# Recurrence of a hybrid layer: the next head's gates and logs one level phase sooner, and the coarsest level's differences inside ScalarE's exponentials

## What is computed

```python
def chunk_recurrence(q, k, v, log_a, s0):
    """S_t = diag(a_t) S_{t-1} + k_t v_t^T ; o_t = S_t^T q_t, chunkwise."""
    ...
    def step(state, blk):
        qc, kc, vc, la = blk
        b = jnp.cumsum(la, axis=2)
        rel = b[:, :, :, None, :] - b[:, :, None, :, :]
        decay = jnp.exp(jnp.where(causal, rel, -jnp.inf))
        ...
            scores = jnp.einsum('bhtsd,bhsd->bhts', qc[:, :, :, None, :] * decay, kc)
        out = (jnp.einsum('bhts,bhsv->bhtv', scores, vc)
               + jnp.einsum('bhtd,bhdv->bhtv', qc * jnp.exp(b), state))
...
def hg_dir(p, z, lb):
    q = jax.nn.silu(to_heads(p[4], HG_HEADS))
    f = lbh + (1.0 - lbh) * jax.nn.sigmoid(to_heads(z, HG_HEADS).astype(jnp.float32))
    return q, 1.0 - f, to_heads(p[7], HG_HEADS), jnp.log(f)
```

## Time and profile before

| what | us |
|---|---|
| median of 3 runs (2803.54 to 2812.65) | 2808.24 |
| the profiled execution | 2807.85 |
| its span, first to last instruction | 2806.2 |
| TensorE busy in the span | 2599.8 |
| VectorE busy | 2061.4 |
| ScalarE busy | 1457.5 |
| GpSimd busy | 587.0 |

### The profile page before, as it was taken

How to read it: one execution, slowest core, us unless ns; L and a number is a source line. 1 busy time by engine, 2 the same in 40 slices (tenths; PEclk the granted TensorE clock), 3 DMA queues, 4 the chain that set the end, 5 groups by cost and what they waited for, 6 DMA issues and landing times. The chain is left out here.

```text
span 2806.2 us, 45616 instructions
## 1 busy us (share of the span) xinstructions
PE 2599.8 (93%) x16249; PEld 2213.0 (79%) x16250; DVE 2061.4 (73%) x2465; ACT 1457.5 (52%) x1498; POOL 587.0 (21%) x457
## 2 busy tenths in 40 slices
PE   7989887999797999999999999999999999999994
PEld 3887665767786789777887978799989897888783
DVE  5265787563665897999879787866686778877884
ACT  5255557212533664776557465544454546645553
POOL 0055666300022211122122111111121112111110
PEclk9998888999898999999999999999999999999997
DMA  7121112171343896999879787866686769967863
GB/s 289 47 69 30 35 33 62 57 260 62 102 104 113 329 380 212 368 355 354 302 234 362 245 302 263 281 202 207 194 295 206 255 228 335 322 210 271 299 229 135
DMA packets 274720, 605.90 MB, mean 216 GB/s; under 512 B 21869, under 2 KB 53013, under 8 KB 273521
## 3 DMA queue, kind: packets, MB, share of 16 engines
q1 hardware_dynamic: 254256, 561.62, 56.2%
q0 software_dynamic: 20384, 43.19, 6.9%
HBM read 582.09 MB, written 46.97 MB: 224 GB/s over the span
## 5 line engine op out<-in xcount | busy, mean ns | idle before, releaser
L2404 ACT ACTIVATE whi<-e_slot 128x2048 fp32r<-128x2048 f32 x296 | 561.0, 1912 | 438.0 <-PE e_acc L2330 370.7
L2466 DVE TENSOR_TENSOR e_slot_r<-e_slot,whi 128x2048 fp32r<-128x2048 f32 x296 | 674.7, 2286 | 101.9 <-ACT whi L2404 101.9
L2327 PE MATMUL e_acc<-e_xhi,whi 128*128 128x256 f32 x1664 | 399.4, 282 | 3.2 <-ACT e_xhi L2408 3.2
L2404 ACT ACTIVATE whi<-slot 128x2048 fp32r<-128x2048 f32 x148 | 283.2, 1914 | 194.1 <-PE e_acc L2302 194.1
L2466 DVE TENSOR_TENSOR slot_r<-slot,whi 128x2048 fp32r<-128x2048 f32 x151 | 344.7, 2285 | 19.5 <-ACT whi L2404 16.5
L2244 POOL DMA_INDIRECT sum<-yo,e_idx_now x50 | 122.4, 2447 | 1014.5 <-issue 541.5
L2300 PE MATMUL e_acc<-whi,e_ahi 128*128 128x512 f32 x800 | 319.3, 399 | 0.0
L2327 PEld LDWEIGHTS e_acc<-e_xhi,whi 128*128 128x128 f32 x1664 | 313.1, 188 | 6.3 <-ACT e_xhi L2408 6.3
L2302 PE MATMUL e_acc<-whi,e_alo 128*128 128x512 f32 x800 | 313.4, 392 | 0.0
L2301 PE MATMUL e_acc<-e_slot_r,e_ahi 128*128 128x512 f32 x800 | 311.5, 389 | 0.0
L2300 PE MATMUL e_acc<-whi,e_xhi 128*128 128x512 f32 x768 | 303.3, 395 | 0.2
(11 more groups left out here) (407 smaller groups left out, 5059.2 us busy)
## 6 DMA issues: line engine op xcount, KB each, us to landing
e_slot<-in_w SPq DMA_DIRECT2D x296, 1024.0 KB, 8.1
slot<-in_w SPq DMA_DIRECT2D x151, 1024.0 KB
rv<-in_w_ada SPq DMA_DIRECT2D x32, 512.0 KB, 5.2
slot<-in_w_in SPq DMA_DIRECT2D x9, 1024.0 KB, 9.9
wa<-in_w_ada SPq DMA_DIRECT2D x8, 1024.0 KB, 17.3
slot<-in_w_in SPq DMA_DIRECT2D x12, 512.0 KB, 4.6
xt<-in_x SPq DMA_DIRECT2D x8, 512.0 KB, 15.0
slot<-in_w_out SPq DMA_DIRECT2D x4, 1024.0 KB, 13.0
```

The source lines that it names most:

```text
L2327: pe.matmul(out[:, c, :], whi[i % RING][:, w], xhi[:, kk, :], start=first, stop=False, skip_group_check=True)
L2404: act.activation(whi[i % RING][:], raw[i % PIECES][:], ACT.Copy).then_inc(S["whi_made"], 1)
L2466: v.tensor_tensor(wlo[i % PIECES][:], raw[i % PIECES][:], whi[i % RING][:].bitcast(F32), ALU.subtract).then_inc(S["wlo_made"], 1)
```

## The change

In `hgrn2`:

- Level 0 (halves of 64) leaves GpSimd. ScalarE's `first_level` takes the exponential straight from the cumulated logs, with the log at the middle of a tile as bias column: 16 instructions of 64 columns for each half, in place of two of 512. For half of them the column must be negated: `middles` on VectorE, four `tensor_scalar` of 4 columns per head.
- The order of the six gate groups becomes `Z_ORDER`: the last 512 columns of both directions first. TensorE does four groups of head h+2, not two, between the updates and the scores of head h+1. For heads 1 and 2 (`ahead`) the last two groups and both queries come after the fourth score block.
- ScalarE, for the same heads: the sigmoids and logs of direction 0 stand before the second level phase, those of direction 1 behind its level 2; `roots(h, 0)` moves from level 3 to behind the phase.
- VectorE, for the same heads: `cumulate` and `keys` of the next head stand inside the phase, the decayed keys between the last masks.
- Chunk 3h+7 is loaded and split ahead of the query decays; in head 0 that is chunk 7, which goes where the query weights (chunk 5) are.
- Turned keys use bank `ps[0]` in place of `po`; both chains of states come before level 6 of the first phase.

Its core:

```diff
@@ hgrn2: banks and names
+        middle = t.sb("h_middle", [P, 2, 2, LT])
...
-        tb = [t.ps("h_tb"), po]
-        ups = ps + tb
+        tb = [t.ps("h_tb"), ps[0]]
+        ups = [ps[1], ps[2], po, ps[3], tb[0], ps[0]]
...
+        Z_ORDER = [(0, 2), (1, 2), (0, 0), (0, 1), (1, 0), (1, 1)]
...
@@ SyncE
             load_chunk(3)
+            load_chunk(4)
             for h in range(HEADS):
                 if h + 1 < HEADS:
-                    load_chunk(3 * h + 4)
                     load_chunk(3 * h + 5)
                     if h + 2 < HEADS:
                         load_chunk(3 * h + 6)
+                        if h:
+                            load_chunk(3 * h + 7)
                     load_values(h + 1)
+                    if h == 0:
+                        load_chunk(7)
@@ TensorE, main loop
                 if more:
-                    gates_of_keys(h + 1, 2 if h else 0)
+                    gates_of_keys(h + 1, 4 if h else 0)
...
                 output(h, HT - 1)
                 if more:
-                    for i in range(3 if h else 1, 6):
+                    for i in range(5 if h else 1, 6):
                         gates_of_keys(h + 1, i)
+                    if h:
+                        queries(h + 1, 0)
+                        queries(h + 1, 1)
...
-                if more:
+                if more and h == 0:
                     queries(h + 1, 0)
+                elif more:
+                    turn_keys(h + 1, 0)
                 output(h, LT - 1)
                 if more:
-                    queries(h + 1, 1)
-                    for n in range(6):
+                    if h == 0:
+                        queries(h + 1, 1)
+                    for n in range(1 if h else 0, 6):
                         turn_keys(h + 1, n)
                     updates(h + 1)
                     if h + 2 < HEADS:
-                        gates_of_keys(h + 2, 0)
-                        gates_of_keys(h + 2, 1)
+                        for i in range(4):
+                            gates_of_keys(h + 2, i)
@@ ScalarE
+            def first_level(h, half):
+                act.wait_ge(S["s_done"], LT * h + half * HT)
+                act.wait_ge(S["middles"], 4 * (h + 1))
...
+                for i in range(HT):
+                    mf, mb = fwd[:, i, 0, HALF_TILE - 1:HALF_TILE], bwd[:, i, 1, 0:1]
+                    act.activation(k4[:, i, 0], fwd[:, i, 0], ACT.Exp, scale=-1.0, bias=mf)
+                    k = act.activation(k4[:, i, 1], bwd[:, i, 1], ACT.Exp, bias=middle[:, h % 2, 1, half * HT + i:half * HT + i + 1])
+                k.then_inc(S["lev_exp"], 1)
...
             for h in range(HEADS):
                 more = h + 1 < HEADS
-                if more:
+                ahead = h > 0 and more
+                if ahead:
+                    for i in (2, 3):
+                        copy_z(h + 1, i)
+                    high_chunk(3 * h + 5)
+                    logs(h + 1, (0,))
+                elif more:
                     high_chunk(3 * h + 4)
-                    for i in range(2):
-                        copy_z(h + 1, i)
...
                 for l in range(NL):
                     levels(h, 1, (l,))
-                    if l == 3:
+                    if l == 3 and not ahead:
                         roots(h, 0)
-                    if more and l in (0, 1, 3, 5):
-                        copy_z(h + 1, (2, 3, None, 4, None, 5)[l])
+                    if ahead and l in (0, 1):
+                        copy_z(h + 1, 4 + l)
+                    elif ahead and l == 2:
+                        logs(h + 1, (1,))
+                    elif more and not ahead and l < 6:
+                        copy_z(h + 1, l)
...
+                if ahead:
+                    roots(h, 0)
+                    key_decays(h + 1)
+                    if h + 2 < HEADS:
+                        high_chunk(3 * h + 6)
+                        high_chunk(3 * h + 7)
+                    query_sig(h + 1, 0)
+                    query_sig(h + 1, 1)
+                    roots(h, 1)
+                elif more:
...
+                    query_sig(h + 1, 1)
+                    high_chunk(3 * h + 6)
+                    high_chunk(3 * h + 7)
...
@@ GpSimd
-                    levels(h, 1, range(NL))
+                    levels(h, 1, range(1, NL))
...
-                    levels(h + 1, 0, range(1))
+                    levels(h + 1, 0, range(1, 2))
                     query_decays(h + 1)
-                    levels(h + 1, 0, range(1, NL))
+                    levels(h + 1, 0, range(2, NL))
@@ VectorE, main loop, for the heads with ahead (1 and 2)
+                        if ahead and l == 0:
+                            cumulate(h + 1, 0)
+                        elif ahead and l == 1:
+                            keys(h + 1, 0)
+                        elif ahead and l == 5:
+                            cumulate(h + 1, 1)
+                            keys(h + 1, 1)
                     pick(h, HT)
+                    if ahead:
+                        finish(h, 0)
+                        pick(h, HT + 1)
+                        decayed_keys(h + 1, 0)
+                        pick(h, HT + 2)
+                        decayed_keys(h + 1, 1)
+                        pick(h, HT + 3)
...
-                        if l == NL - 2:
-                            states(h + 1, 0)
-                    states(h + 1, 1)
+                        if l in (4, 5):
+                            states(h + 1, l - 4)
```

110 lines of the change are left out of this document (73 added, 37 removed).

## The result

| | before | after |
|---|---|---|
| median, 20 runs each | 2806.22 us (2802.12 to 2812.69) | 2813.42 us (2809.36 to 2817.74) |
| ratio | | 1.0022, 95% interval 1.0017 to 1.0028 |
| profiled execution, span | 2806.2 us | 2811.5 us |
| TensorE, VectorE, ScalarE, GpSimd busy | as shown ahead | 2585.6, 2051.8, 1479.8, 560.4 us |

The change costs 7.2 us. That is a slowdown clear of the noise of twenty runs, and under the 0.3% (8.4 us) that I had drawn as a line. The forecast was 2818, range 2799 to 2830, with 0.48 for slower by over 0.3% and 0.40 for within 0.3%; the second is what came, and not the one that I held more likely.

What follows compares the result with a forecast made beforehand. No engine fills a head; each head is a loop of waits, and the wait ending last in a piece decides. Terms +14.1 + 0.6 - 3.8 - 0.7 = +10.2 us gave 2818 us, range 2799 to 2830.

Steps and rivals of the forecast that it cites:

- The signs that the prediction had named as right: Head 1's scores 13 to 15 us later, ScalarE idle 3 us for chunk 7, short exponentials 0.24 us apart, among others.
- those that it had named as wrong: A VectorE wait ahead of head 1's scores, head 1 under 88 us, or short exponentials under 0.15 us apart.
- Head 0 to head 1: From head 0's first scores to head 1's: chunk 7, short exponentials and four gate groups cost +14.1 us.
- the first term: Ahead of head 1's updates: ScalarE's wait for chunk 7's load and its copy cost 4.1 us (bounds 3.3 and 6).
- Head 1 to head 2: From head 1's first scores to head 2's: updates end sooner, gate groups take longer, 94.1 against 93.5 us, +0.6 us.
- Head 2 to head 3: From head 2's first scores to head 3's: VectorE reaches its low parts at 82 us, not 85.7; -3.8 us (0 to -7).
- Head 3: Last head: level 0 comes sooner, but TensorE had waited only 0.66 us there; -0.7 us.
- I add to the first and let the second stand: Baseline: terms are added to the profiled 2807.85 us; the median of the runs stays 0.4 above it.
- No change: Rival, chance 0.34: all terms at lower bounds, head 0 costs 11.1, head 1 gains 3, head 2 gains 7; +0.4 us, 2808.
- half-way value of +5: In the no-change rival: total with the terms' values half way, +5 us, still inside 0.3%.
- The faster rival: Chance 0.12: the VectorE-GpSimd port decides, heads 1 and 2 each win some 12 us; total -10.6, 2797 us.
- The worse one: Rival, chance 0.17: chunk 7 +1.5, exponentials +1.8 in heads 0 and 1, head 1's phase 3 later; 2826 to 2830.

Runs made afterwards that it cites:

- chunk7_late: The changed kernel with chunk 7's high and low parts made behind the turned keys of head 1, not ahead of the query decays: 2809.30 us, ratio 1.0006.
- before_again: The kernel before, unchanged, profiled a second time: 2802.24 us.
- pool_level0: The changed kernel with level 0 given back to GpSimd, everything else as changed: 2817.87 us, ratio 1.0027 to the kernel before.
- delay: The kernel before with a chain of 30 tiny reciprocals on VectorE ahead of head 3's low parts of the row weights: 2811.85 us, ratio 1.0021.
- split_late_gate: split_keys_queries with the output gate's sigmoid, and so GpSimd's gate products, moved behind the first two copies of the next gates: 2794.57 us, ratio 0.9954.
- fold_only: The kernel before with only level 0's differences folded into ScalarE's exponentials: 2800.13 us, ratio 0.9966.
- split_keys_queries: fold_only with the 16 short exponentials split: keys' 8 behind turned keys 1, queries' 8 behind turned keys 3, levels 1 and 2 later: 2799.82 us, ratio 0.9981.

## Why the prediction was right, and where it was not

The signs that the prediction had named as right all came, and none of those that it had named as wrong.

**Head 0 to head 1 (+14.1 forecast).** It measured +13.4 on the clock of the profile, +13.6 as a piece. Right in each step: chunk 7 cost 4.18 us (4.1), the short exponentials were 0.24 us apart (0.24), the updates ended at 301.66 (301.8), the four groups took 19.09 us (19.6), the scores came at 320.75 (321.4). Of the two prices for a short exponential the one from the rows stood: 3.82 us for sixteen, where the budget of the Trainium skill (ScalarE: Activation LUTs, "Rules for kernel authors"), taken as 0.35 us each without overlap, made 5.6. VectorE was done at 310.3 and nobody waited for it. chunk7_late confirms the first term by itself. Three small readings were off and moved nothing: the updates before ended at 295.05 (294.44 and 0.61), not 294.9; the fifth block before started at 344.93, not 344.6; and the lower bound of 6.7 us for the groups comes out as 6.95 (19.4 less 8.5 and 3.95).

**Head 1 to head 2 (+0.6).** Right against the profile that I worked from (+1.2), and each landmark within 1.5 us: level 0 on VectorE 13.0 us after the first scores (12.9), the end of the phase 41.2 (39.7), updates 75.5 (74.5), then 19.1 (19.6). What failed is the base: 93.4 us is one draw of a piece that took 90.3 in before_again. Over two profiles each the term is +3.3.

**Head 2 to head 3 (-3.8).** The sign was right and the size too large: -1.6, or -2.6 over two profiles. "The updates end 74.5 us after the head's first scores" was 76.9, and VectorE reached the low parts 83.8 us after them instead of 82. ScalarE, then VectorE in the kernel after:

```profile
492.36 3.71 ACT L818 ACTIVATE h_early<-slot 128x2048 fp32r<-128x2048 f32 x2 [4.74 <-PE h_ps L689]
```

```profile
496.62 0.43 DVE L1196 TENSOR_TENSOR h_wk<-h_wk,h_keyA 128x256 f32<-128x256 f32 x1 [6.12 <-ACT h_wk L936]
...
499.17 4.48 DVE L1143 TENSOR_TENSOR slot_r<-slot,h_early 128x2048 fp32r<-128x2048 f32 x2
```

The step that I had named did it: ScalarE's high parts of the row weights wait 4.74 us for the updates, level 3 stands behind them, and VectorE waits 6.12 us.

**Head 3 (-0.7).** -0.9.

**The sum.** The terms make +10.2 and the recurrence lost 12.3 us in the same profile. The total moved by 5.3 there and by 7.2 in the medians, since 6.7 us less passed behind the recurrence. "I add to the first and let the second stand" took for granted that the rest of the program takes the same time. This step failed, and its miss of 6.7 outweighed the 2.1 by which the terms were too small. In the second pair of profiles the recurrence ends 15.0 us later and the span is 7.4 longer: 2.7 of the difference lie in the retention stage and 5.6 behind it, less 0.7 ahead of it. That the change itself wins this time back is not shown. What lies behind the recurrence scattered over 11.5 us in the fourteen profiles (2246.4 to 2257.9), its longest value came with the changed order of gates (pool_level0), and delay, an edit of the old order, ended 5.0 us shorter behind it too. Nor is it shown that all of it is chance, for the medians of twenty runs also moved by less than either pair of recurrences. A higher clock in the retention stage is seen, its cause isn't.

**The rivals.** No change (0.34) asked for heads 1 and 2 to gain 10 us; they gained 0.4 in the one pair of profiles, and nothing over both. The measured +7.2 lies beside that rival's half-way value of +5, but not by its path: the terms were not at their lower bounds, the rest of the program was shorter. The faster rival (0.12) had its condition written down, updates within 62 us of the head's first scores; they took 75.5. Its mechanism is real all the same: split_late_gate won from it, at another place, where VectorE stood beside the gate products and not beside the subtractions. The worse one (0.17) is refuted in its terms: chunk 7 landed as priced, the exponentials overlapped, and the phase of head 1 ended 1.5 us later than I had it, not 3.

**The story of the change in one line.** Early gates and logs bring the updates of a head to 75.5 us after its first scores where it was 80.4, 4.9 us won (2.7 against before_again, where it was 78.2); the groups that pay for it add 6.1 (19.1 against 13.0) behind them, head 0 pays 14 without having anything from it, and the fold, the one part that won 9.5 us alone, adds nothing measurable to the rest.

## What to carry to other kernels

Take a change with several parts apart before judging it: here the good part was worth 9.5 us alone and nothing measurable beside the others, which had hidden one wait that it removes and put others in its place. In an in-order queue, ask of work moved earlier what stands behind it: the gates that were moved into a wait of 4 us were 11 us long, and they did not fill the wait but replaced it. And when the last arrivals at a point are within a microsecond of each other, as TensorE and VectorE in fold_only, shorten both in one experiment: splitting the exponentials alone won nothing over fold_only, and with the gate products out of VectorE's way as well the kernel is 12.9 us under the one before, 3 us beyond fold_only, which the intervals do not yet separate. And look whether a test of a delay delays only what it means to: here the delayed work ran into another engine's and was 8.1 us late, not 5.95.

## What the runs showed of the hardware that was not expected

A VectorE multiplication of two tensors in SBUF took 2.28 us beside GpSimd's gate product, and its twin 0.41 us behind it; it ended 0.3 us after the GpSimd instruction did. The same 0.3 us stand between the two ends in before (2.34 us long), before_again (2.33) and fold_only (2.62), and at head 2 of split_keys_queries (2.58), wherever in GpSimd's instruction the multiplication began. The state updates just before, which take one operand from PSUM, kept their 0.38 us each while GpSimd ran the other gate product. So the slowdown is no mere sharing of bandwidth: VectorE stood until GpSimd's instruction was over. The Trainium skill (SBUF — State Buffer, "SBUF: two separate sides") speaks of an exclusive lock held for a whole instruction, and these rows agree with it.

Two executions of one unchanged program differed by 3.3 us at the end of the recurrence, and the retention stage took one of three times (60.1, 62.3 to 63.0, 65.3 us), with a mean granted clock of 0.91, 0.85 to 0.89, and 0.83. A term of 1 to 3 us read from a single profile is no better than that.
